# Norm sums of the FFN moved between the products of the second pair, and another VectorE and ScalarE order at two seams

## The reference, cut to what matters

```python
x = x + y                                   # residual of the token mixer
hn = _rms_norm(x, norm_ffn[l])              # x * rsqrt(mean(x*x) + eps) * gain
gate, up = jnp.split(hn @ w_gate_up[l], 2, axis=-1)
x = x + (jax.nn.silu(gate) * up) @ w_down[l]
...
y = _rms_norm(x, norm_final)
```

## Time and profile before

| | us |
|---|---|
| median of 3 runs | 1835.62 |
| lowest, highest | 1834.9, 1837.39 |
| the profiled execution, its own time | 1834.62 |
| its span in the trace | 1832.6 |
| TensorE matmul busy | 1776.0 |
| VectorE, ScalarE, GpSimd busy | 762.0, 495.9, 884.5 |

### The profile page before, as it was taken

How to read it: one execution, slowest core, us unless ns; L and a number is a source line. 1 busy time by engine, 2 the same in 40 slices (tenths; PEclk the granted TensorE clock), 3 DMA queues, 4 the chain that set the end, 5 groups by cost and what they waited for, 6 DMA issues and landing times. The chain is left out here.

```text
span 1832.6 us, 29793 instructions
## 1 busy us (share of the span) xinstructions
PE 1776.0 (97%) x12218; PEld 1734.8 (95%) x12218; DVE 762.0 (42%) x804; ACT 495.9 (27%) x896; POOL 884.5 (48%) x452
## 2 busy tenths in 40 slices
PE   7999999999999999999978998999999999999997
PEld 6999999999999999998978997999999999999997
DVE  4153535351222123225357687445445444533213
ACT  6011111100411145465001125444444443201003
POOL 3424242334334333332436547888888886345440
PEclk9999999999999999999989998999999999999999
DMA  6211121224222252436444332222222222723212
GB/s 242 76 61 58 60 67 50 81 73 161 87 79 86 86 176 85 154 127 167 124 147 133 114 128 81 70 69 69 92 91 77 83 69 87 256 81 120 62 40 104
DMA packets 172610, 186.58 MB, mean 102 GB/s; under 512 B 7401, under 2 KB 148705, under 8 KB 172553
## 3 DMA queue, kind: packets, MB, share of 16 engines
q1 hardware_dynamic: 140560, 132.58, 22.7%
q10 hardware_dynamic: 31993, 53.20, 8.6%
HBM read 131.99 MB, written 53.76 MB: 101 GB/s over the span
## 5 line engine op out<-in xcount | busy, mean ns | idle before, releaser
L822 PE MATMUL unit_ps<-a_hi,w_part 128*128 128x344 f32 x3888 | 779.0, 326 | 9.0 <-DVE a_lo L1734 3.9
L822 PEld LDWEIGHTS unit_ps<-a_hi,w_part 128*128 128x128 f32 x3888 | 634.0, 189 | 19.3 <-issue 13.9
L719 POOL TENSOR_TENSOR w_part<-w_raw,consts 128x1024 fp32r<-128x1024 f32 (+1 forms) x98 | 231.4, 2362 | 780.9 <-PE unit_ps L822 761.9
L822 PE MATMUL unit_ps<-a_lo,w_part 128*128 128x344 f32 x1944 | 413.0, 321 | 0.0
L822 PEld LDWEIGHTS unit_ps<-a_lo,w_part 128*128 128x128 f32 x1944 | 328.9, 189 | 0.0
L721 POOL TENSOR_TENSOR w_part<-w_raw,w_part 128x1024 fp32r<-128x1024 f32 (+1 forms) x98 | 253.4, 2586 | 7.7
L1147 PE MATMUL pair_ps<-a_hi,slots_a 128*128 128x258 f32 x1056 | 177.5, 283 | 2.9 <-DVE a_lo L2117 1.6
L1147 PEld LDWEIGHTS pair_ps<-a_hi,slots_a 128*128 128x128 f32 x1056 | 148.5, 189 | 3.3 <-DVE a_lo L2117 1.8
L1710 DVE TENSOR_TENSOR stage<-unit_ps,rstd 128x1032 f32<-128x1032 f32 x42 | 51.7, 1232 | 208.3 <-PE unit_ps L822 208.3
L822 PE MATMUL unit_ps<-b_hi,w_part 128*128 128x344 f32 x720 | 134.2, 320 | 3.4 <-DVE b_lo L2109 3.4
L822 PEld LDWEIGHTS unit_ps<-b_hi,w_part 128*128 128x128 f32 x720 | 116.9, 188 | 4.5 <-DVE b_lo L2109 4.0
(11 more groups left out here) (250 smaller groups left out, 2501.6 us busy)
## 6 DMA issues: line engine op xcount, KB each, us to landing
w_raw<-in_w_in SPq DMA_DIRECT2D x58, 512.0 KB, 3.8
h_spill<-h_out SPq DMA_DIRECT2D x11, 1032.0 KB, 5.0
raw_a<-in_w_gate_up SPq DMA_DIRECT2D x11, 1024.0 KB, 6.9
raw_b<-in_w_gate_up SPq DMA_DIRECT2D x11, 1024.0 KB, 5.1
att_spill<-stage ACTq DMA_DIRECT2D x18, 516.0 KB, 2.7
att_in<-att_spill ACTq DMA_DIRECT2D x3, 3072.0 KB, 11.2
gate_spill<-stage ACTq DMA_DIRECT2D x16, 516.0 KB, 3.6
a_lo<-h_spill SPq DMA_DIRECT2D x15, 516.0 KB, 5.0
```

The costliest lines, as they stand in the source:

```text
L719: pool.tensor_tensor(part[:, 0], raw, one, ALU.mult).then_inc(w_high, 1)
L822: mm = pe.matmul(unit_ps[s][:, n, 0:PIECE], w_part[:, slot, w, k0 + k, :], x[:, k, n * PIECE:(n + 1) * PIECE], start=(k == 0 and part == 0 ...
```

## The change

Seven edits, all of them of order; no matmul, vector or scalar operation is added or left out, except that a loop body of ScalarE is written out once.

1. The four norm sums move from pair (0, 0) to pair (0, 1): two between its products 0 and 1, two between 1 and 2. They write the r banks instead of z_ps[1].
2. TensorE's wait for the four roots moves from ahead of pair (0, 1) to ahead of its product 3.
3. On ScalarE the roots move behind the weight parts of pair (0, 1), around the snapshot of its product 0; the first round of the ScalarE loop is written out for this.
4. ScalarE makes the weight part of product 2 of pair (0, 0) before the snapshot of product 0.
5. VectorE adds the square of residual tile 6 not ahead of the residual of tile 7 but behind its sums.
6. VectorE makes combine 0 of pair (0, 1) ahead of the reciprocal.
7. At the second seam VectorE makes the eight row_lows ahead of the last combine.

```diff
@@ norm_sum @@
-                end(pe.matmul(z_ps[1][:, j % 2, 0:QUAD], const("ones"), rstd[:, j * QUAD:(j + 1) * QUAD], start=True, stop=True), j)
+                end(pe.matmul(r_ps[:, j % 2, 0:QUAD], const("ones"), rstd[:, j * QUAD:(j + 1) * QUAD], start=True, stop=True), j)
@@ pair @@
-                if start and x == 1:
-                    for b in range(2):
-                        pe.wait_ge(task_free[b], T_END // 2)
...
+                elif normed_pair:
+                    combos_by(t, x, 0)
+                    for j in range(2):
+                        norm_sum(j)
                 else:
                     combos_by(t, x, -1)
                 product(t, x, 1, ...)
+                if normed_pair:
+                    for j in range(2, 4):
+                        norm_sum(j)
                 snaps_by(t, x, 1)
                 product(t, x, 2, ...)
-                if not first_pair:
+                if normed_pair:
+                    for b in range(2):
+                        pe.wait_ge(task_free[b], T_END // 2)
+                elif not first_pair:
                     combos_by(t, x, 0)
...
-                if first_pair:
-                    for j in range(2):
-                        norm_sum(j)
                 combos_by(t, x, 1)
                 product(t, x, 5)
                 if first_pair:
-                    for j in range(2, 4):
-                        norm_sum(j)
@@ scalar @@
+            part(0, 0, 2, False)
             snapshot(0, 0, 0)
-            part(0, 0, 2, False)
...
             snapshot(0, 0, 3)
-            norm_root(Place(T_NORM2), (0, 1))
-            part(0, 1, 3)
-            norm_root(Place(T_NORM2), (2, 3))
-            for s in range(4, PRODUCTS):
+            for s in range(3, PRODUCTS):
                 part(0, 1, s)
...
+            def pair_steps(t, x, following, rooted=False):
+                if rooted:
+                    norm_root(Place(T_NORM2), (0, 1))
                 snapshot(t, x, 0)
+                if rooted:
+                    norm_root(Place(T_NORM2), (2, 3))
...
+            pair_steps(0, 1, (1, 0), True)
+            pair_steps(1, 0, (1, 1))
@@ vector @@
-                add_square(m)
                 dve.wait_ge(s_raw, k + 1)
                 if m < KT - 2:
+                    add_square(m)
...
             dve.tensor_tensor(s4, a12, s2, ALU.subtract).then_inc(s_raw, 1)
+            add_square(m - 1)
             dve.wait_ge(a_ready, 2 * KT + m + 1)
...
                 if start:
+                    combine(t, 1, 0, h_out)
                     norm_factor(T_END)
...
-                for n in range(COMBOS):
+                for n in range(1 if start else 0, COMBOS):
+                    if between and n == COMBOS - 1:
+                        between()
                     combine(t, 1, n, h_out)
-                if between:
-                    between()
```

More of the change, by code:

```diff
@@ L1163, in pair @@
                     pe.wait_ge(unit_free[0], U_DOWN // 2)
-                if start and x == 1:
-                    for b in range(2):
-                        pe.wait_ge(task_free[b], T_END // 2)
-                first_pair = start and x == 0
+                first_pair, normed_pair = start and x == 0, start and x == 1
                 product(t, x, 0, ready=(a_ready, [2 * KT + 1 + k for k in range(KH)]) if first_pair else None)
@@ L1231, in norm_root @@
                     full(pl, j)
-                    empty(act.activation(rstd[:, j * n:(j + 1) * n], z_ps[1][:, j % 2, 0:n], ACT.Sqrt, scale=1.0 / D,
+                    empty(act.activation(rstd[:, j * n:(j + 1) * n], r_ps[:, j % 2, 0:n], ACT.Sqrt, scale=1.0 / D,
                                          bias=const("eps")[:, 0:1]), j)
@@ L1640, in silu @@
                     act.activation(temp[:, j, :], temp[:, j, :], ACT.Silu).then_inc(gate_silu, 1)
-            def pair_steps(t, x, following):
+            def pair_steps(t, x, following, rooted=False):
+                if rooted:
+                    norm_root(Place(T_NORM2), (0, 1))
                 snapshot(t, x, 0)
+                if rooted:
+                    norm_root(Place(T_NORM2), (2, 3))
                 if following:
@@ L1659, in pair_steps @@
                         part(*following, s)
-            with act.Fori(0, PAIRS_FF - 1) as t:
-                pair_steps(t, 1, (t + 1, 0))
-                pair_steps(t + 1, 0, (t + 1, 1))
+            pair_steps(0, 1, (1, 0), True)
+            pair_steps(1, 0, (1, 1))
+            with act.Fori(0, PAIRS_FF - 2) as t:
+                pair_steps(t + 1, 1, (t + 2, 0))
+                pair_steps(t + 2, 0, (t + 2, 1))
             pair_steps(PAIRS_FF - 1, 1, None)
@@ L2227, in gate_pair, with up_pair @@
                     dve.tensor_tensor(temp[:, j, :], temp[:, j, :], rstd[:], ALU.mult).then_inc(gate_ready, 1)
-            def up_pair(t, between=None):
-                for n in range(COMBOS):
+            def up_pair(t, between=None, start=False):
+                for n in range(1 if start else 0, COMBOS):
+                    if between and n == COMBOS - 1:
+                        between()
                     combine(t, 1, n, h_out)
-                if between:
-                    between()
                 dve.wait_ge(combined, t * (2 * COMBOS) + 2 * COMBOS)
@@ L2243, in _ @@
             gate_pair(0, True)
-            up_pair(0)
+            up_pair(0, start=True)
             with dve.Fori(0, PAIRS_FF - 2) as t:
```

## The result

The changed kernel takes **1842.43 us** (median of 7 runs, 1841.28 to 1842.97) against 1837.12 us of the kernel before (7 runs, 1834.90 to 1837.73): a ratio of 1.003 [1.002, 1.004], so 5.3 us slower. Timed again later with the experiments it stood at 1.0028 [1.0018, 1.0039] to the kernel before. The forecast was 1841.8 us, inside a range from 1837.0 to 1846.0.

The account below looks back on a forecast made before the run. TensorE, busy 97% of the span, and its gaps were taken as the bound. −0.6 + 9.8 − 2.8, less 0.2, made +6.2 on 1834.62, so 1840.8; 1.0 for the median gave 1841.8 us, range 1837.0 to 1846.0.

Parts of the forecast that it names:

- The wall at the first seam: Pair (0, 0): VectorE's last square ends where it did, 0 us, between −2 and +2; product 5 waits for combine 0.
- The rival in which VectorE slips out of GpSimd's way: Before the last square: each VectorE instruction going fast takes off 1.08 us, all nine giving 1832.1; chance 0.05.
- The rival of a later wall: First seam: the moved square and three more VectorE instructions pay 1.08 us each, nothing regained: +4.3, 1846; chance 0.11.
- The rival in which product 5 doesn't need combine 0: First seam: the 5.3 us gap and its slow clock go, as the change says: 1834; chance 0.03.
- Slow clock at the first seam: Behind the gap of some 6 us ahead of product 5: the half clock costs the same 2.6 us as before.
- T: The start of pair (0, 1), forecast at 1130.9 instead of 1131.55, −0.6 us.
- Pair (0, 1): Reciprocal at T + 8.0, product 4 at T + 19.0 after standing still 6.1 us, plus slow clock: +9.8 us.
- The term for the clock: Pair (0, 1), behind product 4's new wait: the slow clock once more, 2.6 us.
- The step that carried the forecast's sign: Pair (0, 1): product 4 waits for a snapshot behind both silus; reciprocal to product 4 stays 11.02 us.
- The rival without a second fall of the clock: Pair (0, 1): the clock doesn't fall behind the new wait: +3.6 us, 1839.2; chance 0.12.
- Second seam: First down unit starts earlier without a slow clock, losing 0.5 us to a late third tile: −2.8 us, at least −1.0.
- The sum: Whole kernel: −0.6 + 9.8 − 2.8 = +6.4, less 0.2 for the multiplications: +6.2 us.

Follow-up runs that it names:

- start_only: The kernel before with edits 4 and 5 alone: 1836.05 us, ratio 1.0000 to the kernel before.
- move_only: The kernel before with edits 1, 2, 3 and 6, without 4, 5 and 7: 1843.28 us, ratio 1.0037 to the kernel before.
- combine_early: The changed kernel with combine 0 of pair (0, 0) ahead of the last two remainders and last square on VectorE: 1837.06 us, 1.0006 to the kernel before.
- silu_late: The changed kernel with both silus of pair (0, 1) behind the snapshots of products 2 and 3 on ScalarE: 1833.75 us, 0.9985 to the kernel before.
- filler: The changed kernel with 40 unused matmuls ahead of product 4 of pair (0, 1): 1840.24 us, ratio 1.0022 to the kernel before.
- seam2_only: The kernel before with edit 7 alone: 1832.79 us, ratio 0.9982 to the kernel before.
- both_fixed: The changed kernel with the edits of combine_early and silu_late together: 1830.26 us, ratio 0.9967 to the kernel before.

## Why the prediction was right, step by step

- **The wall at the first seam held.** The last square ended 26.12 us after the pair's start, before 25.87 (26.10 in start_only and 25.85 in move_only, so edits 4 and 5 cost the 0.2 us); product 5 came right behind combine 0, as foreseen, 0.5 us earlier. The rival in which VectorE slips out of GpSimd's way fell: the hole of GpSimd came (2.01 us, two remainders at 0.68 us in it), but only those two went fast, and the square moved into GpSimd's stretch took 2.34. The rival of a later wall fell too. The rival in which product 5 doesn't need combine 0 fell by its wait, and combine_early showed it from the other side. GpSimd's row of that hole:

```profile
1114.42 3.15 POOL L761 TENSOR_TENSOR slots_b<-mixed,slots_b 128x512 fp32r<-128x512 f32 x2 [2.01 <-ACT slots_b L1590]
```

- **Slow clock at the first seam: mis-sized.** This is the largest error of the sum. I let the gap of 6 us cost the 2.6 us of the old one. From product 5 to T are 7.50 us, 5.78 of them products: 1.7. It is 7.53 in the second execution of the changed kernel, where the gap was 6.5 us and product 4 had run at full clock (in the first, the clock of 1116 to 1122 was 0.75, ahead of the gap, and cost nothing). So it is not the slow product ahead that made it cheap. What differs from before is that product 5 follows the gap directly, and not behind two norm sums; why the clock comes back sooner is open.
- **Pair (0, 1): right in its waits.** Reciprocal at T + 8.3 (8.0), product 4 at T + 18.95 (19.0), its wait 5.5 us (6.1; TensorE reaches it at T + 13.4, not T + 12.9), clock 0.50 behind it. Reciprocal to product 4 took 10.65 us and not 11.02, as the multiplications took 2.38 and not 2.76, and that made up for the late reciprocal. The term for the clock was 2.1 us, not 2.6. The step that carried the forecast's sign, that all of the chain behind the reciprocal moves with it and the snapshot stands behind the silus, is shown by silu_late.
- **The rival without a second fall of the clock** fell by the row of 0.50, and filler priced it.
- **Second seam: too careful by 0.5 us.** I let TensorE lose 0.5 us to a late third tile. It didn't come to that in this execution (the wait is 0.3 us in all; in seam2_only 0.4 us were lost there), and the clock stayed up:

```profile
1564.00:1576.00 12.00, 11.72 (x82) 11.54 (x81) 9.59 (x9) 8.55 (x8) 0.08 (x1) 1.00 1.03 391
```

  Of the 3.3 us gained there, 1.7 are the wait that went. The other 1.5 are the clock, and move_only, with the wait and without the fall, shows that not every execution pays them.
- **The sum** was +6.2, by the trace +4.5, by the medians +5.1 to +5.3. The errors (0.7, 0.5 and 0.5) all have one sign: each came in the main from giving a clock fall or a late tile the full price of the nearest row. That 1841.8 lies within 0.6 us of the measured 1842.43 is in part luck: the kernel before came out 1.5 us higher over seven runs (1837.12) than over the three that the forecast started from (1835.62), and this made up for a difference forecast 0.9 us too large.
- **Slips of reading that changed little.** The last two matmuls of product 4 take 0.24 us together, not each; the sum, 1116.26, is right. 9.80 less 7.14 is 2.66, not 2.6. And pair (0, 1) took 20.64 us before, not 20.5: the next pair starts at 1152.19, as product 4 began with a slower matmul pair (0.51 us).

What failed was in the experiments' expectations: for combine_early and both_fixed I removed the two long gaps on paper and did not ask what ScalarE's queue makes the freed sums wait for.

## What to carry to other kernels

Moving work that TensorE waited for to a later place moves everything that hangs on it as well: write down the chain behind it (here 10 us from the reciprocal to a snapshot) and look for the short instruction at its end that somebody else needs. Before giving up such a move, reorder the queues it meets: with the silus behind the snapshots, the combine ahead of the last square and the roots ahead of weight parts, the same move went from 0.3% slower to 0.5% faster. And compare two traces from an event just ahead of the edit, not by their spans: here the spans said 7.4 us and the anchored stretch 4.5.

## What the runs showed that I had not expected

- The start of pair (0, 0) varies by 4.3 us over eleven profiled executions, though TensorE's program ahead of it is the same in all, while the stretch behind it repeats within 0.1 us in the two executions of the changed kernel.
- The clock's price for one gap isn't fixed: 2.6 us before (two sums first), 1.7 at the same place in the changed kernel, 2.1 behind the snapshot. At the second seam the same wait of 2.0 us cost 1.5 us of clock in the kernel before and nothing in move_only. Useless matmuls in a wait that can't be avoided took the fall away (2.0 us) without delaying the product behind it.
- A fall can come before a gap is long: 1116 to 1122 ran at 0.75 in one execution of the changed kernel (product 4 of pair (0, 0) took 4.33 us), and 1114 to 1120, the same work two microseconds earlier, at 1.00 in another (3.04 us), behind the same waits of 0.5, 1.6 and 1.7 us. It lay ahead of the wall and so cost nothing. The Trainium skill, "TensorE: Matmul & The Clock Gate", section "Part 1: The HAM clock gate (the "warmup" mystery)", says that how much work meets the low clock at a kernel's start differs from run to run; these rows show the same in the middle of one:

```profile
1116.00:1122.00 6.00, 4.48 (x24) 4.26 (x24) 6.00 (x4) 2.35 (x5) 6.00 (x3) 0.75 0.19 55
```

```profile
1114.00:1120.00 6.00, 3.12 (x24) 2.91 (x24) 6.00 (x4) 2.30 (x5) 5.99 (x3) 1.00 0.21 62
```

- The 19 table loads and 24 us that ScalarE saved over the whole loop are not to be seen in the time.
